# Both input products of a head ahead of its gate panel, conditioning turns moved, and rotary sums on the key's side

## The reference, cut to what matters

```python
# first block
u = rmsnorm(h, norm_mix);  u_ssm, q, k, v = split(u @ w_in)
y_ssm  = s5_branch(u_ssm, ...)            # diagonal state space, 32 groups of 64 states, glu
y_attn = stick_breaking_attention(q, k, v)  # 8 heads of 64
gates  = sigmoid(u @ w_gate + b_gate)
h = h + (g_ssm * (y_ssm @ w_up_ssm) + g_attn * (y_attn @ w_up_attn)) @ w_out
h = h + relu(rmsnorm(h) @ w_ff1)**2 @ w_ff2
# second block, two layers; shift, scale, gate = split(silu(c) @ w_ada + b_ada)
u = h * (1 + scale) + shift;  proj = u @ w_in_2
a: glu, causal convolution of width 31, layer norm, silu;   b: gated convolution of width 3
q = rms_norm(q_lat) @ w_uq               # 8 heads, 64 without and 32 with rotary part
q_pe, k_pe = apply_rope(q_pe), apply_rope(k_rope)   # k_pe is shared by the heads
o = causal softmax attention;  h = layer_norm(ALPHA*h + gate * (merged branches @ w_o))
# apply_rope(x): [x1*cos - x2*sin, x2*cos + x1*sin]
```

## Time and profile before

| | |
|---|---|
| median of three runs | 1257.37 us |
| profiled execution | 1257.67 us |
| its span, first to last instruction | 1255.9 us |
| mean granted clock of TensorE | 0.909 |
| PE busy | 1097.3 us, 87% |
| DVE busy | 762.3 us, 61% |
| ACT busy | 536.6 us, 43% |
| POOL busy | 253.0 us, 20% |
| the chain that ended last | PE 58%, DVE 23%, issue 7%, ACT 7%, POOL 3% |

### The profile page before, as it was taken

The page is one execution under the profiler, slowest core; times in us unless marked ns, Lnnn a source line. Parts: engine busy times, 40 slices in busy tenths (PEclk is TensorE's granted clock), DMA queues, the critical chain, the costliest instruction groups (busy, mean ns, idle before and its releaser), DMA issues.

```text
span 1255.9 us, 19600 instructions
## 1 busy us (share of the span) xinstructions
PE 1097.3 (87%) x8120; PEld 1012.5 (81%) x8120; DVE 762.3 (61%) x1111; ACT 536.6 (43%) x613; POOL 253.0 (20%) x125
## 2 busy tenths in 40 slices
PE   5989779788989999979968798999799688989995
PEld 4976557667889999969867698998688687889985
DVE  4947556655353523255687788665556977795652
ACT  4533334253244444345423363643465132635432
POOL 2094753000078878700000000000000000000000
PEclk7977797788989999989979899999899788999998
DMA  7532332165566565545523345464447142545610
GB/s 250 186 102 90 112 125 77 68 201 180 167 195 197 168 200 169 182 128 190 172 68 101 101 143 161 136 213 153 131 139 235 38 131 76 160 137 166 202 35 33
DMA packets 159431, 179.53 MB, mean 143 GB/s; under 512 B 4976, under 2 KB 141680, under 8 KB 159344
## 3 DMA queue, kind: packets, MB, share of 16 engines
q1 hardware_dynamic: 159024, 177.22, 44.6%
q0 software_dynamic: 320, 1.07, 0.2%
HBM read 177.23 MB, written 1.05 MB: 142 GB/s over the span
## 4 chain that ended last, share of the span: by engine, by line
PE 58%; DVE 23%; issue 7%; ACT 7%; POOL 3%; DMA 1%; DVEq 0%; SPq 0%; ACTq 0%; POOLq 0%
PE pg L1573 17%; PE pg L1574 16%; PE pg L1575 16%; DVE area L1473 7%; DVE area L1091 5%; ACT w_hi L803 3%; DVE w_lo L1082 3%; ACT area L782 2%; DVE area L1099 2%; PE p_y L1729 1%; PE p_s L1663 1%; DVE mx L1494 1%; PE p_s L1712 1%; DVE area L1109 1%; DMA raw<-in_w_in 1%
## 5 line engine op out<-in xcount | busy, mean ns | idle before, releaser
L1573 PE MATMUL pg<-u_hi,w_hi 128*128 128x256 f32 x1664 | 497.7, 299 | 40.3 <-DVE u_lo L1091 36.0
L1574 PE MATMUL pg<-u_lo,w_hi 128*128 128x256 f32 x1664 | 487.3, 293 | 0.0
L1575 PE MATMUL pg<-u_hi,w_lo 128*128 128x256 f32 x1664 | 486.3, 292 | 0.0
L1573 PEld LDWEIGHTS pg<-u_hi,w_hi 128*128 128x128 f32 x1664 | 336.5, 202 | 53.0 <-issue 44.7
L1574 PEld LDWEIGHTS pg<-u_lo,w_hi 128*128 128x128 f32 x1664 | 336.8, 202 | 0.8
L1575 PEld LDWEIGHTS pg<-u_hi,w_lo 128*128 128x128 f32 x1664 | 335.9, 202 | 0.0
L1082 DVE TENSOR_TENSOR w_lo<-raw,w_hi 128x2048 fp32r<-128x2048 f32 (+3 forms) x109 | 241.2, 2218 | 115.0 <-ACT w_hi L803 114.8
L803 ACT ACTIVATE w_hi<-raw 128x2048 fp32r<-128x2048 f32 (+2 forms) x147 | 272.5, 1857 | 79.7 <-issue 38.6
L711 POOL TENSOR_TENSOR w_lo<-raw,w_hi 128x2048 fp32r<-128x2048 f32 x38 | 175.9, 4646 | 220.5 <-ACT w_hi L803 220.5
L809 ACT ACTIVATE area<-pg 128x512 f32<-128x512 f32 (+2 forms) x92 | 54.0, 587 | 168.9 <-PE pg L1575 156.9
L1473 DVE SCALAR_TENSOR_TENSOR area<-area,par 128x256 f32<-128x256 f32 x240 | 97.8, 479 | 0.8
(11 more groups left out here) (211 smaller groups left out, 1338.3 us busy)
## 6 DMA issues: line engine op xcount, KB each, us to landing
raw<-in_w_in SPq DMA_DIRECT2D x68, 1024.0 KB, 5.5
raw<-in_w_ff SPq DMA_DIRECT2D x32, 1024.0 KB, 5.6
raw<-in_w_ada SPq DMA_DIRECT2D x24, 1024.0 KB, 5.2
raw<-in_w_gate SPq DMA_DIRECT2D x8, 1024.0 KB, 7.7
...
```

The costliest lines, as they stand in the source:

```text
L1573: pe.matmul(dst, w_h, x_h, start=first, stop=False)
L1574: pe.matmul(dst, w_h, x_l, start=False, stop=False)
L1575: return pe.matmul(dst, w_l, x_h, start=False, stop=last_)
```

## The change

In the head loop `bu` 2m+2 stands directly behind `bu` 2m+1 and ahead of the gate panel. `s5_y` f-1 moves from even heads, behind `s5_out`, to odd heads ahead of the gate panel, and `s5_inner` behind `state` 2m+1; `s5_gelu` goes to the next even head, and the last of each to head 8 and behind it. Behind the loop, conditioning panel 10 and the turns of 9 and 10 stand between the two up_attn panels. Turn 12, panel 13 and its turn stand behind the first panels of w_out.

The rotary step is replaced. The scores are sums over 128 rows instead of 96: the rotary rows of a query head stand twice, from columns of w_uq that are copied twice when they are split, and are multiplied by cosine and by sine (`rope_q`, two DVE operations). The key's rows hold the rotated key and the same rotated once more by `rot` (`rope_k`, one matmul, three DVE operations), which POOL spreads over the eight heads. `rope_k` stands behind `latent_norm`, `rope_q` behind the panel ukv and ahead of the convolution. `scores` waits for `k_spread` as well. The waits for p_c and p_o that `rope` had go to `turn` and `context` of head 0. The sine tables fill 64 rows (one more ACT and one more DVE operation), two small loads of frequencies and two more selects on POOL are at the start.

The diff, cut to its core:

```diff
@@ -171,36 +179,41 @@
             step("stick_scores", m + 1)
         if m < HEADS:
             step("bu", 2 * m + 1)
-            panel("gate", 0, m, "w_gate", 0, 256 * m, KT, 256, 1)
         if 2 * m + 2 < PAIRS:
             step("bu", 2 * m + 2)
+        if m % 2 and f:
+            step("s5_y", f - 1)
+        if m % 2 == 0 and f >= 2:
+            step("s5_gelu", f - 2)
+        if m < HEADS:
+            panel("gate", 0, m, "w_gate", 0, 256 * m, KT, 256, 1)
         if m:
             step("s5_out", m - 1)
-        if m % 2 == 0 and f:
-            step("s5_y", f - 1)
+        if m == HEADS:
+            step("s5_y", WT - 1)
+            step("s5_inner", WT - 1)
         if m < HEADS:
             step("state", 2 * m + 1)
+        if m % 2 and f:
+            step("s5_inner", f - 1)
         if m in (2, 4):
             step("table", f + 1)
-        if m % 2 == 0 and f:
-            step("s5_inner", f - 1)
         if m:
             step("stick_out", m - 1)
-        if m % 2 and f:
-            step("s5_gelu", f - 1)
         if m < HEADS:
             ada_panel(m + 1)
             step("ada_take", m + 1)
     step("split", "ctx")
     ada_panel(9)
     step("ada_take", 9)
+    step("s5_gelu", WT - 1)
+    step("split", "y")
+    panel("up_attn", 0, 0, "w_up_attn", 0, 0, WT, 512, 2)
+    step("ada_turn", 9)
     ada_panel(10)
-    step("s5_gelu", WT - 1)
-    step("ada_turn", 9)
     step("ada_take", 10)
+    panel("up_attn", 0, 1, "w_up_attn", 0, 512, WT, 512, 2)
     step("ada_turn", 10)
-    step("split", "y")
-    half("up_attn", 0, "w_up_attn", D)
     half("glu", 0, "w_glu", W)
     ada_panel(11)
     step("glu_mul")
...
@@ -211,13 +224,15 @@
     ada_panel(12)
     step("split", "u1")
     step("ada_take", 12)
-    step("ada_turn", 12)
-    ada_panel(13)
-    step("ada_take", 13)
-    step("ada_turn", 13)
-    step("ada_end", 0)
     for n in range(4):
         panel("out", 0, n, "w_out", 0, 256 * n, KT, 256, 1)
+        if n < 2:
+            step("ada_turn", 12 + n)
+        if n == 0:
+            ada_panel(13)
+            step("ada_take", 13)
+        if n == 1:
+            step("ada_end", 0)
         if n:
             norm_sums(1, n - 1)
     norm_steps(1, "u2", 14)
...
@@ -256,6 +271,7 @@
         else:
             step("ln_affine", l - 1)
         step("latent_norm", l)
+        step("rope_k", l)
         wide("a2", l, "w_in_2", A2, W)
         step("split", ("ql", l))
         step("split", ("kvl", l))
@@ -263,11 +279,11 @@
         for n in range(2):
             panel("uq", l, n, "w_uq_2", 0, 4 * QK * n, QL // P, 4 * QK, 2)
         panel("ukv", l, 0, "w_ukv_2", 0, 0, KVL // P, 1024, 6)
+        step("rope_q", l)
 
         parts = iter(range(2 * CONV_PARTS))
         for _ in range(6):
             step("conv_a", l, next(parts))
-        step("rope", l)
         wide("cg", l, "w_in_2", CG, W)
         between = [(job, at, n) for job, at in (("xb", XB), ("gc", GC), ("gb", GB), ("bg", BG), ("ag", AG)) for n in range(2)]
         for h in range(HEADS + 2):
...
@@ -562,7 +578,18 @@
         def slot(tensor, q):
 
             n = q["index"] % RAW if tensor is raw else q["s"] % HL
-            return tensor[:, n, 0:q["kt"] * q["cols"]].rearrange("p (k n) -> p k n", k=q["kt"])
+            cols = q["cols"] if tensor is raw else twice(q["cols"]) if q["job"] in TWICE else q["cols"]
+            return tensor[:, n, 0:q["kt"] * cols].rearrange("p (k n) -> p k n", k=q["kt"])
+        def halves_of(q, tensor):
+            if q["job"] not in TWICE:
+                n = q["kt"] * q["cols"]
+                at = q["index"] % RAW if tensor is raw else q["s"] % HL
+                return [tensor[:, at, 0:n]]
+            wide = QK if tensor is raw else P
+            a = slot(tensor, q).rearrange("p k (h m) -> p (k h) m", m=wide)
+            return [a[:, :, 0:QK], a[:, :, NOPE:QK] if tensor is raw else a[:, :, QK:P]]
 
 
 
...
@@ -661,7 +688,11 @@
             pool.dma_start(par[:, :], t["params"]).then_inc(sem("par_landed"), 16)
             pool.dma_start(bst, t["b_state"]).then_inc(sem("s5_landed"), 16)
             pool.dma_start(ct, t["c_state"]).then_inc(sem("s5_landed"), 16)
-            pool.dma_start(pos[NOPE:QK, :], t["positions"].partition_broadcast(ROPE)).then_inc(sem("pos_landed"), 16)
+            pool.dma_start(pos[NOPE:P, :], t["positions"].partition_broadcast(2 * ROPE)).then_inc(sem("pos_landed"), 16)
+            for i in range(2):
+                at = NOPE + ROPE * i
+                pool.dma_start(freq[at:at + ROPE, :], t["params"][NOPE:QK, COL["inv_freq"]:COL["inv_freq"] + 2]
+                               ).then_inc(sem("pos_landed"), 16)
             pool.memset(ones[:, :], 1.0).then_inc(*c.event("const", "ones"))
             pool.memset(nones[:, :], -1.0).then_inc(*c.step())
             pool.memset(ident[:, :], 0.0).then_inc(*c.step())
...
@@ -766,7 +799,12 @@
                 if f == 0:
                     signs()
 
-            steps = dict(panel=panel, gate_ahead=panel, s5_diag=s5_diag, table=table)
+            def rope_k(l, _):
+                pool.wait_ge(sem("k_roped"), over("k_roped", l))
+                pool.tensor_copy(kf[NOPE:P, :, :], spread(kpe[NOPE:P, :], 2 * ROPE, HEADS, T)).then_inc(*event("k_spread", l))
+            steps = dict(panel=panel, gate_ahead=panel, s5_diag=s5_diag, table=table, rope_k=rope_k)
             for kind, a, b in ORDER:
                 if kind in steps:
                     steps[kind](a, b)
...
@@ -906,13 +945,13 @@
                 elif job == "kv_lat":
                     take(g, kv_lat, both)
                 elif job == "k_rope":
-                    take(g, kpe[NOPE:QK, :], pg[g % 2][NOPE:QK, 0:T])
+                    take(g, kpe[NOPE:P, :], pg[g % 2][NOPE:P, 0:T])
                 elif job == "a2":
                     take(g, acc[:, 2 * n:2 * n + 2, :], both, ACT.Sigmoid)
                 elif job == "uq":
                     for i in range(2):
                         a = 4 * n + 2 * i
-                        take(g + i, qf[0:QK, a:a + 2, :], pair(pg[(g + i) % 2][0:QK, :]))
+                        take(g + i, qf[:, a:a + 2, :], pair(pg[(g + i) % 2][:, :]))
                 elif job == "ukv":
                     for i in range(4):
                         take(g + i, kf[0:NOPE, 2 * i:2 * i + 2, :], pair(pg[(g + i) % 2][0:NOPE, :]))
...
@@ -1077,10 +1117,10 @@
                     if q["s"] >= HL:
                         past = SPLIT[q["s"] - HL]
                         dve.wait_ge(sem("groups"), past["g"] + past["groups"] - 1 + 1)
-                    n = q["kt"] * q["cols"]
-                    r, s = q["index"] % RAW, q["s"] % HL
-                    dve.tensor_tensor(w_lo[:, s, 0:n], raw[:, r, 0:n], w_hi[:, s, 0:n].bitcast(F32),
-                                      ALU.subtract).then_inc(sem(f"raw_free{r}"), 1)
+                    parts = list(zip(halves_of(q, w_lo), halves_of(q, raw), halves_of(q, w_hi)))
+                    for i, (dst, src, hi) in enumerate(parts):
+                        ins = dve.tensor_tensor(dst, src, hi.bitcast(F32), ALU.subtract)
+                        ins.then_inc(*((sem(f"raw_free{q['index'] % RAW}"), 1) if i == len(parts) - 1 else c.step()))
 
             def split_ahead(n, _):
                 low_halves(first_splits(n, ahead))
...
@@ -1439,23 +1480,26 @@
                         stt(x[:, j, :],
                             x[:, j, :], col((name, l), j), rstd[:, which, :], ALU.mult, ALU.mult).then_inc(*(c.event("rows", ("ql" if which == 0 else "kvl", l), 0) if j == n - 1 else c.step()))
 
-            def rope(l, _):
-                rows = slice(NOPE, QK)
-                wide = [ROPE, 2, T]
-                sin2, cos2 = spread(rsin[rows], *wide), spread(rcos[rows], *wide)
-                dve.wait_ge(sem("rotated"), over("rotated", l, 0))
-                tt(kpr[rows, :], p_y[rows, 0:T], rsin[rows], ALU.mult).then_inc(*c.step())
-                tt(kpe[rows, :], kpe[rows, :], rcos[rows], ALU.mult).then_inc(*c.step())
-                tt(kpe[rows, :], kpe[rows, :], kpr[rows, :], ALU.add).then_inc(*c.step())
-                copy(kf[rows, :, :], spread(kpe[rows, :], ROPE, HEADS, T)).then_inc(*c.step())
-                for i in range(4):
-                    b = (p_bu, p_z, p_c, p_o)[i]
-                    a = slice(2 * i, 2 * i + 2)
-                    dve.wait_ge(sem("rotated"), over("rotated", l, 1 + i))
-                    tt(rtmp[rows, :, :], pair(b[rows, :]), sin2, ALU.mult).then_inc(*c.step())
-                    tt(qf[rows, a, :], qf[rows, a, :], cos2, ALU.mult).then_inc(*c.step())
-                    tt(qf[rows, a, :], qf[rows, a, :], rtmp[rows, :, :], ALU.add).then_inc(*(c.event("roped", l) if i == 3 else c.step()))
+            def rope_k(l, _):
+                rows = slice(NOPE, P)
+                dve.wait_ge(sem("rotated"), over("rotated", l))
+                if l:
+                    dve.wait_ge(sem("k_spread"), over("k_spread", l - 1))
```

(37 more changed lines are left out.)

54 lines of the change are left out of this document (31 added, 23 removed).

## The result

The changed kernel takes 1210.62 us (median of 4 runs, 1208.45 to 1214.46) against 1257.46 us for the kernel before on the same chip: a ratio of 0.963, 95% interval 0.961 to 0.966, 46.8 us less. Its profiled execution took 1214.46 us, span 1212.6; it is the slowest of the four. The forecast was 1199, with a range of 1188 to 1222.

The account below looks back on a forecast made before the run. TensorE's dear waits all end on VectorE, in the head loop and at the rotary step. 40.5 - 1.4 + 3.5 + 16 - 0.7 = 58 us off the profiled 1257.7 gave 1199, range 1188 to 1222.

Parts of the forecast that it names:

- head loop: Heads 0 to 7: VectorE runs state(2m+1) beside the gate panel, heads take about 15.3 us; 40.5 us gained, bounds 5 to 44.5.
- behind the loop, to the end of up_ssm: Late last state and turns, an earlier up_attn start, turns and conditioning between its panels: -1.4 us, bounds -5 and +2.
- before and in w_out: out(0) starts at 306.4 at the high clock, less 2.1 for turns and panel put behind: +3.5 us, bounds 1 and 4.
- rotary, both layers: Second block's attention: 2.5 us in place of 11.5 on VectorE's chain per layer; 16 us gained, bounds 5 and 18.
- feed-forward (forecast for the tables alone): A third sine and one more VectorE operation under the feed-forward: -0.7 us, at most 1.
- the main case: The forecast's terms hold as summed, 1190 to 1206 us; chance 0.60.
- A: Head loop: the clock falls in most heads, 2 to 5.6 us in 7 heads, about 1217 us in total; chance 0.13.
- B: Head loop: VectorE is the bound after all, heads of 16.5 us, 8 us more, 1208 us in total; chance 0.12.
- the signs named ahead: Heads 15.3 to 16 us apart, clock 1.00 through the loop; wrong if period over 17 or second block under 10 shorter.
- C: Attention stage: TensorE's panels and ScalarE's splits take the rotary gain back, about 1213 us in total; chance 0.08.
- D: Head loop: the clock never recovers, heads of 29.8 us, slower than before at 1292 us; chance 0.03.
- E: Head loop: TensorE and VectorE stay coupled, only rotary and w_out gain, 1239 us in total; chance 0.04.

Follow-up runs that it names:

- The two halves: The changed kernel with only the second input product back behind the gate panel, 1213.79 us; or with only the output sums (s5_y) back, 1239.8 us.

## Why the prediction was right, and where its sizes were off

The forecast was 58.2 us from profile to profile, measured were 43.3. The mechanism of the two large terms held, and one small term carries half of the difference:

| term | forecast, us | measured, us |
|---|---|---|
| head loop | 40.5 | 42.5 |
| behind the loop, to the end of up_ssm | -1.4 | -9.4 |
| before and in w_out | 3.5 | 0.6 |
| rotary, both layers | 16 | 15.5 |
| feed-forward (forecast for the tables alone) | -0.7 | -2.1 |
| between the layers, and the end | not in the sum | -3.8 |

The median of 1210.62 lies within the stated range, but outside the main case's own 1190 to 1206. It is the width that was taken in for the rivals A and B that holds it, and neither of them is what happened; that part is luck. Of the signs named ahead, the second block is shorter by 11.7 us, near the 10 that would have counted as wrong, one head (4) takes 17.6 us, and the clock did not stay at 1.00 through the loop.

- *The head loop:* forecast 40.5, measured 42.5, and 45.9 at the same place with the loop alone, where the first panel of all starts 1.5 us earlier and the clock falls in two heads and not in three. Within it errors cancel, and so its nearness to 40.5 is partly luck. The quiet head is 14.5 us, not 15.27, since the two input products, now side by side, overlap: from 122.17 to the panel at 123.60 is 1.43 us for both, where the earlier trace rows have 1.13 and 1.12; it also spares their seams. The Trainium skill (TensorE: Matmul & The Clock Gate, Part 3: Packing small matmuls) says that matmuls with few rows run side by side in the array when their operands lie in different row groups; these two have 32 rows each from different strips, and the rows at 122.58 and 122.70, which overlap, agree. Over six heads that is 4.6 us. Against it: sums(1) at 102.25 and not 101.5; three falls of the clock, 1.5 us each, 4.5 against the 4 taken; 1.42 us ahead of head 4's sums; and 0.87 in the same head for the state that the early input product needs, which the forecast had as 0.9 once. (The other 1.71 of p_bu's waits is head 0's, also foreseen.) VectorE's part of a quiet head was 12.6 to 12.9 us; the forecast said 13.5 to 14.5, where its own terms add to 13.3 to 13.9.
- *The coupling:* the forecast named the wait of s5_y, ahead of state(2m+1) on VectorE. The two halves show it: without the late s5_y 27.0 us of p_c's wait remain, 24.1 of them in the loop.
- *The tail, the step that failed in size:* forecast -1.4, measured 33.1 - 42.5 = -9.4. The late state(15) was foreseen, as 2.5 us; it cost about 3 at the turn, and up_attn then did not start when its forecast said, as s5_out(7) behind that turn ran at the low clock (3.6 us for 1.9) and va_lo came 3.14 us after PE asked. Up to up_attn's start the forecast had -2.5 + 3.4 = +0.9; measured are 40.85 - 42.53 = -1.7. The inserted panel and turns cost 2.9 against 2.3. What the sum did not have is the load: I counted the instructions of the moved conditioning panel, its bank wait and its turns, but not that its place in a ring of four slots sets when the panel four further on can be loaded. That is 3.84 us at glu, and behind it 7.5 us for glu and not 5.9, at the low clock. Moving that panel by one place won 4.8 us back, leaving the early split out about 4 more.
- *Before w_out:* forecast +3.5, measured 33.7 - 33.1 = +0.6. u_lo came when forecast and out(0) ran in 6.2 us, but out(1) waited 1.51 us, again with a low half ahead of the sum in VectorE's queue (the load of a w_out panel), and then ran at the low clock, 7.5 us. The bound of 1 for the low clock was in the text; the wait was not. Where the clock held, the same order was worth 2.0 to 2.4 us.
- *Rotary:* forecast 8.4 and 7.7, measured 40.0 - 31.6 = 8.4 and, from the first panel of layer 1 on, 44.1 - 37.0 = 7.1, the same two figures with the rotary change alone. The 7.7 leaves out the 0.6 for PE's rotation of the key that the 8.4 has; with it the sum gives 7.1. The key's operations are 0.43 us each, the query's two 2.48 together, and in layer 1 the wait at a1 is 1.40 against 0.56. The copy of 4.0 us on GpSimd and the split of the weights in parts are hidden.
- *Feed-forward:* 2.1 us, of which the forecast had 0.7 for the tables; with the rotary change alone it is 0.6. The other 1.5 us are the second to fourth panels, 18.9 us from start to start against 17.4 for the same matmuls, at a mean granted clock of 0.91 against 1.00. The longer waits for GpSimd's low halves (3.1 us in two, 1.5 before) cost little: the first stands behind a panel that ran faster by as much, the second costs 0.5.
- *Not in the forecast:* 3.0 us between the attention of layer 0 and layer 1, and 0.8 at the end. The order of the work is the same there. The 3.0 came out as 2.9 in the kernel with the loop alone, which has the old second block, and in the one with the rotary change alone. So neither part of the change is its cause. Between xb and w_o the same matmuls were busy for 191.20 us and not 189.19, and w_o's first two panels took 14.4 for 13.2. The one execution profiled of the kernel before had the higher clock (0.96 and 0.93, against 0.95 and 0.87 in these two stretches); why is open.
- *The rivals:* falls of the clock (A) came, but not in most heads; waits for VectorE (B) in the loop were 1.71, 1.42 and 0.87, 4 us and not 8; the rotary gain stayed (C); D and E are refuted by heads of 14.5 us.
